# The prompt attention's side jobs laid over five tiles of the delta recursion instead of four

## What is computed

```
def dilated_attention(q, k, v, q_idx):            # mixer B, 6 heads x 64; prompt: 512 queries
    ...
        s = jnp.einsum('bqhd,bqmhd->bhqm', q, kg).astype(jnp.float32) * scale
        ...
        e = jnp.exp(s - m)
        den = jnp.sum(e, axis=-1, keepdims=True)
        outs.append(jnp.einsum('bhqm,bqmhd->bqhd', (e / den).astype(v.dtype), vg))
...
def gated_delta(q, k, v, g, beta, s0, chunk):     # mixer C, 6 heads x 64, chunks of 64 tokens
    ...
    sol = lax.linalg.triangular_solve(a_mat + jnp.eye(chunk, dtype=jnp.float32), rhs,
                                      left_side=True, lower=True, unit_diagonal=True)
    ...
    def step(s, inp):
        u_p = uu - jnp.einsum('bhcd,bhde->bhce', ww, s)
        o = jnp.einsum('bhcd,bhde->bhce', qd, s) + jnp.einsum('bhij,bhje->bhie', aa, u_p)
        s = gt[..., None, None] * s + jnp.einsum('bhcd,bhce->bhde', kd, u_p)
        return s, o
```

## Time and profile before

| | us |
|---|---|
| median of 3 runs | 1873.63 (1867.89 to 1884.23) |
| the profiled execution, its own time | 1871.8 |
| its span in the profile | 1869.9 |
| PE busy in the span | 1551.6 (83%) |
| DVE, ACT, POOL busy | 626.6, 399.7, 148.2 |

### The profile page before, as it was taken

One profiled execution on the slowest core, in us unless ns is written; L12 is line 12 of the kernel. 1 busy time (PEld: TensorE's weight loads), 2 busy tenths in 40 slices (PEclk: granted clock), 3 DMA queues, 4 the chain that ended last, 5 costly groups with the idle time before them and its releaser, 6 DMA issues. The chain is left out here.

```text
span 1869.9 us, 31394 instructions
## 1 busy us (share of the span) xinstructions
PE 1551.6 (83%) x13036; PEld 1018.1 (54%) x13036; DVE 626.6 (34%) x1625; ACT 399.7 (21%) x967; POOL 148.2 (8%) x185
## 2 busy tenths in 40 slices
PE   6999977887969798888479999788879697988882
PEld 3475666776535455444244766667765354554451
DVE  2442236665312411111234331466652133111114
ACT  3212032231511111111222210333305111111112
POOL 0000000000000022222000000000000001222210
PEclk9999888897889799999779999898969897999996
DMA  7140120002691599999701410300038825999994
GB/s 285 47 146 8 53 97 2 1 2 80 197 325 70 194 378 389 397 399 399 275 28 47 147 37 23 97 2 2 2 79 253 293 93 218 386 392 396 398 394 181
DMA packets 97261, 337.23 MB, mean 180 GB/s; under 512 B 32637, under 2 KB 44157, under 8 KB 72429
## 3 DMA queue, kind: packets, MB, share of 16 engines
q1 hardware_dynamic: 77852, 305.79, 44.8%
q0 software_dynamic: 12464, 25.92, 4.0%
q10 hardware_dynamic: 6816, 3.67, 0.7%
HBM read 313.25 MB, written 37.80 MB: 188 GB/s over the span
## 5 line engine op out<-in xcount | busy, mean ns | idle before, releaser
L1660 PE MATMUL bank<-ring,proj_raw 128*64 128x256 f32 x1536 | 202.2, 418 | 46.0 <-DMA ring<-in_w 44.4
L1401 PE MATMUL bank<-ring,hT_raw 128*128 128x384 f32 (+2 forms) x768 | 227.9, 460 | 0.0
L1401 PEld LDWEIGHTS bank<-ring,hT_raw 128*128 128x128 f32 x768 | 148.3, 194 | 77.3 <-issue 3.3
L1660 PEld LDWEIGHTS bank<-ring,proj_raw 128*64 128x64 f32 x1536 | 126.7, 145 | 106.7 <-issue 57.3
L2303 DVE TENSOR_TENSOR qkv_raw<-qkv_raw,bank 128x128 f32<-128x128 f32 x64 | 18.4, 288 | 433.1 <-ACT qkv_raw L1071 433.1
L1338 PE MATMUL bank<-hT_raw,ring 128*128 128x512 f32 x288 | 128.8, 601 | 0.0
L823 POOL DMA_INDIRECT proj_raw<-h_rows,idx x64 | 61.1, 955 | 667.1 <-DVE idx L1953 395.7
L1565 PE MATMUL bank<-ring,hT_raw 128*128 128x512 f32 x256 | 113.6, 597 | 0.0
L1117 PE MATMUL bank<-work 64*64 64x64 f32 (+1 forms) x1608 | 75.2, 261 | 37.6 <-DVE work L1805 26.2
L1117 PEld LDWEIGHTS bank<-work 64*64 64x64 f32 (+1 forms) x1608 | 68.8, 172 | 47.0 <-DVE work L1805 29.5
L1680 PE MATMUL bank<-ring,proj_raw 128*64 128x512 f32 x384 | 92.9, 604 | 1.3 <-issue 1.3
(11 more groups left out here) (323 smaller groups left out, 2162.5 us busy)
## 6 DMA issues: line engine op xcount, KB each, us to landing
ring<-in_w SPq DMA_DIRECT2D x144, 1024.0 KB, 23.0
work<-in_w SPq DMA_DIRECT2D x32, 1024.0 KB, 21.7
proj_raw<-in_w SPq DMA_DIRECT2D x16, 1024.0 KB, 29.6
ring<-in_w_in SPq DMA_DIRECT2D x10, 1536.0 KB, 16.7
ring<-in_cache_win_k SPq DMA_DIRECT2D x12, 768.0 KB, 8.7
ring<-in_cache_win_v SPq DMA_DIRECT2D x12, 768.0 KB, 11.8
ring<-in_w_out SPq DMA_DIRECT2D x4, 2048.0 KB, 22.1
proj_raw<-y_rows SPq DMA_DIRECT2D x16, 512.0 KB, 7.6
```

The costliest lines, as they stand in the source:

```text
L1401: mm = pe.matmul(bank[0:ROWS[t], 0:w.shape[2]], hT[:, k, 128 * t:128 * t + ROWS[t]], w[:, k, :], start=k == 0, stop=k == KT - 1)
L1660: mm = pe.matmul(bank[CAP * j:CAP * j + CAP, 0:256].rearrange("p (w f) -> p w f", w=2), rowsT[k % 2][:, CAP * c:CAP * c + CAP], w13[:, :, ...
```

## The change

The list of points becomes a list of pairs (tile, point): the 13 points of each of the four prompt tiles as before, then five of the sample tile (points 0, 1, 2, 3 and 10). The 33 slots are spread evenly over 57 points and not over 52. The guards that kept the side jobs out of the sample tile go, in the order of jobs and in the programs of PE, DVE and ACT.

```
--- before.py
+++ after.py
@@ -147,14 +147,14 @@
     return OUT_ORDER.index(t)
 
 
-SIDE_POINTS = tuple(range(11)) + (12, 14)
+SIDE_POINTS = [(t, n) for t in range(NP) for n in tuple(range(11)) + (12, 14)] + [(NP, n) for n in (0, 1, 2, 3, 10)]
 NSIDE = 6 + STEPS + 3
 
 
 def beside(t, point):
 
-    points = NP * len(SIDE_POINTS)
-    at = len(SIDE_POINTS) * t + SIDE_POINTS.index(point)
+    points = len(SIDE_POINTS)
+    at = SIDE_POINTS.index((t, point))
     return [n for n in range(NSIDE) if n * points // NSIDE == at]
 
 
@@ -194,20 +194,18 @@
                 v.extend(jobs[1])
         a += [("cg", t), ("D", t), ("DT", t)]
         v += [("qT", t), ("kT", t), ("bT", t)]
-        if t < NP:
-            side(0)
+        side(0)
         v += [("AA", t), ("AT0", t), ("AT1", t)]
-        if t < NP:
-            side(1)
+        side(1)
         a += [("N2", t)]
         v += [("N2T", t)]
+        side(2)
         if t < NP:
-            side(2)
             a += [("N4", t)]
             v += [("N4T", t)]
         v += [("M1", t)]
+        side(3)
         if t < NP:
-            side(3)
             a += [("N8", t)]
             v += [("M2", t)]
             side(4)
@@ -221,8 +219,8 @@
         v += [("u", t)]
         a += [("wT", t, c) for c in range(2 if t < NP else 1)]
         v += [("qdT", t)]
+        side(10)
         if t < NP:
-            side(10)
             for c in range(2):
                 v += [("wS", t, c), ("S", t, c), ("o", t, c)]
                 side(12 + 2 * c)
@@ -987,14 +985,14 @@
                     def out(label, dst, n=CW, rr=r):
                         bank = get(label)
                         act.activation(dst[0:rr, 0:n], bank[0:rr, 0:n], ACT.Copy).then_inc(s.act_drained, 1)
+                    side(t, 0)
+                    side(t, 1)
+                    out(("N2", t), N2_, CH * w)
+                    side(t, 2)
                     if t < NP:
-                        side(t, 0)
-                        side(t, 1)
-                    out(("N2", t), N2_, CH * w)
+                        out(("N4", t), N4_)
+                    side(t, 3)
                     if t < NP:
-                        side(t, 2)
-                        out(("N4", t), N4_)
-                        side(t, 3)
                         out(("N8", t), N2_)
                         side(t, 4)
                         if t:
@@ -1015,6 +1013,7 @@
                         root(o_ss)
                         act.activation(ET_[:, 0:192].rearrange("p (g n) -> p g n", g=3)[:, :, 0:NS],
                                        bank[:, 0:3 * NS].rearrange("p (g n) -> p g n", g=3), ACT.Copy).then_inc(s.act_drained, 1)
+                        side(t, 10)
 
                 act.wait_ge(s.vec_drained, V_AT[("S4", 2)] + 1)
                 for g in range(3):
@@ -1442,7 +1441,7 @@
                             pe.matmul(bank[:, 0:128 * (u + 1)], qTb[g][p0_:p0_ + 64, 128 * u:128 * u + 128],
                                       kTb[g][p0_:p0_ + 64, 0:128 * (u + 1)], start=True, stop=True).then_inc(done, 1)
                 for t in range(NT):
-                    delta_tile(pe, s, t, job, after, tr, lambda point, t=t: side(t, point) if t < NP else None)
+                    delta_tile(pe, s, t, job, after, tr, lambda point, t=t: side(t, point))
 
                 def cached(n, b):
 
@@ -2191,7 +2191,7 @@
                             dve.tensor_scalar(a_max[:, j:j + 1], a_max[:, j:j + 1], -1.0, None, ALU.mult).then_inc(s.probs_asked, 1)
                 delta_prepare(dve, s, 0, then)
                 for t in range(NT):
-                    delta_vec(dve, s, t, then, get, kept, inv_root, lambda point, t=t: side(t, point) if t < NP else None)
+                    delta_vec(dve, s, t, then, get, kept, inv_root, lambda point, t=t: side(t, point))
 
                 def own_heads(G):
```

## The result

The change makes the kernel slower: 1898.53 us (median of 4, 1896.09 to 1903.46) for 1872.42 us (median of 4), a ratio of 1.0134 with a 95% interval of 1.0100 to 1.0168. A second measurement beside the experiments gave 1.0124 (1.0090 to 1.0158). I had said 1893 us. Each ratio is to the kernel before, run beside it, and counts undisturbed executions only, which are all but three of the twelve of the kernel with 28 transposes, so it can differ a little from the ratio of the medians.

A forecast was written before the change was run, and what follows sets the result against it. It took the delta stage as bound by its chain from PE to DVE or ACT and back. Prices of 7.0 us a layer, 14 in both, plus 5 for the clock made 19 us: 1893 from the median, range 1879 to 1907.

The forecast's parts named there:

- The mechanism: Delta stage: side jobs move between free and paid places; tile 1 +2.6 us, tile 2 -0.65, tile 3 +3.9 a layer.
- The prices: Cost of a side job at each point: free at 1, 5 (tiles 1 to 3), 10; elsewhere the job less 0 to 0.7 us.
- Point 4: M2 to T: the whole job is paid, as DVE's side job stands ahead of delta_norm and waits for PE; 1.88 us.
- point 9: X to wS: the job less 0.3 us, since DVE's part stands ahead of delta_prepare; 1.4 for slot 28.
- The sample tile: Slots 31 at point 1 and 32 at point 3 cost 1.1 to 2.8 us a layer, 2.4 taken.
- the faster rival: Filled gaps keep PE at full clock in the sample tile, 10 us a layer back: 1868 us; chance 0.05.
- The clock: PE falls to half clock after long idle times: 2.5 us a layer, between -1 and 8; 5 in both.
- The rival to which I had given 0.40: The clock adds nothing, only the prices count: 1882 to 1888 us, centre 1886; chance 0.40.
- The transfers: Cache load 8 in SP's queue goes out at about 454 for 445.54, with 24 us of cover left: no cost.
- the late load: Cache load 8 comes over 24 us late, the sample attention waits and the time passes 1905 us; chance 0.01.
- made up behind: The loss is made up behind the stage, because loads of weights wait for something else: 1874 us; chance 0.05.
- The signs I had named: Tile 3 longer by 4 to 8 us, tile 2 shortest, M2 to T above 7, idle before N2 3.8, delta_norm over 1 later.

The follow-up runs named there:

- the kernel with 28 transposes: Changed kernel plus 28 identity transposes in PE's idle time at point 1 of tiles 1 and 3 and point 5 of tile 1: 1878.70 us, ratio 0.9999.
- The second trace: Trace of the changed kernel measured once more, with no edit: 1893.89 us, ratio 1.0124 to the kernel before.
- the slots at paid places: Kernel before, with the eight slots of tiles 1 to 3 each at points 2, 3, 4, 6, 7, 9, 12, 14: 1920.15 us, ratio 1.0254.
- the layout with one slot at point 5: Slots put where the chain waits anyway, with the second slot at point 5 moved away; against the kernel before: 1834.93 us, ratio 0.9818.
- two slots: Slots put where the chain waits anyway, two at once at points 1 and 5 of tiles 1 to 3; against the kernel before: 1842.64 us, ratio 0.9828.

## Why the prediction was right, point by point

**The mechanism.** Right. The kernel lost where I had said, in tiles 1 and 3, and gained in tile 2; that the sample tile or the spread as such costs is out. With the clock taken out the stages are 5.8 and 6.2 us longer than before, for the 7.0 of my sum.

**The prices.** Right within 0.8 us a tile. With the same rule (0.4 of the half time as loss) the changed kernel's tiles give bare lengths of 56.13 - 8.9 - 6.7 = 40.5 (tile 1), 47.48 - 4.65 - 2.7 = 40.1 (tile 2) and 60.54 - 8.1 - 11.6 = 40.8 (tile 3, all layer 1), the 40.4 to 40.6 of before. In layer 0 they are 39.8, 40.1 and 40.5. (The two tiles of before that the prediction leaves out, 2 and 3 of layer 0, give 40.0 and 40.4, so its agreement to 0.2 was partly luck.) Two readings are off. Point 4 costs what I said, but mostly by DVE's own work and only by a third through DVE's wait for PE. And point 9: X to wS took 1272.54 - 1265.02 = 7.52 us in tile 1 for my 5.63 + 1.4 = 7.03, so nothing of the job (1.7) is hidden there:

```profile
1265.02 0.92 PE L1116 MATMUL bank<-work 64*64 64x64 f32 x24 [0.59 <-ACT work L987]
...
1272.54 1.28 PE L1215 MATMUL bank<-state,ring 128*64 128x64 f32 x12 [3.16 <-DVE ring L1810]
```

**The sample tile.** Mis-sized: 2.4 us a layer taken, 0.3 and 2.9 measured (34.55 and 37.15 for 34.24 and 34.25), and the kernel that moves only the last two slots gained nothing and lost nothing. The second trace has the same two lengths. I had priced both slots at half clock. Where the clock stayed at half throughout (PEclk 0.50) they cost 2.9, about my upper bound of 2.8; in the other layer it came back by the end of slot 31, N2 behind it took 0.94 us for the 1.48 of before, and they cost 0.3. That is a piece of what I had given to the faster rival. The sign that I named for it, `delta_norm` begun over 1 us later, came in one layer only: counted from the tile's start 10.58 us became 10.90 in layer 0, and 10.59 became 13.51 in layer 1. So all of the longer sample tile lies ahead of `delta_norm`.

**The clock.** The term that was too small, and the step of the prediction that was furthest off. I took 2.5 us a layer. The half time of the two stages was 2 x 0.18 x 231.08 + 2 x 0.16 x 227.37 = 156 us before and 2 x 0.17 x 235.69 + 2 x 0.22 x 248.14 = 189 after; 0.4 of the difference is 13 us, with some 2 us open by PEclk's two digits, for my 5. The prices make the other 12, for my 14. So the clock was 8 us too little and the prices 2 too much. For the clock I had no better than a guess between -1 and 8 us a layer, 6.5 was measured, and that the sum still fell into the range is due to the width that I had given to this term. The rival to which I had given 0.40, that the clock adds nothing and the time is 1882 to 1888, is out, with 13 of the 25 us of the stages the clock's. Layer 0 shows no clock loss and layer 1 nearly all of it, and the other way round in the second trace, so where the clock falls stays a matter of chance. That filling a gap can take a fall away is shown; what else decides is open. One reading of mine was wrong: behind 2.53 us of idle time the clock did not come back within N2, it had never fallen. The row of that stretch has PEclk 1.00:

```profile
1333.29:1334.90 1.61, 1.61 (x48) 1.00 0.05 10
```

In layer 0 the same N2 behind the same 2.53 us took 2.47.

**The transfers.** Right. Cache load 8 went out at 456.85 (I had said 454) and at 1403.72, and the next issue at 481.79:

```profile
456.85 0.80 SPq L670 DMA_DIRECT2D hT_raw<-in_cache_win_k  x2
...
481.79 0.55 SPq L711 DMA_DIRECT2D qkv_raw<-in_w_group  x1
```

Behind the stage of layer 0 PE's waits are those of before, the longest for the values, 13.7 us after and 13.1 before (14.3 and 12.7 in layer 1):

```profile
PE bank L1508 <- DMA proj_raw<-in_cache_win_v: 13.7, 1, 13.7
```

```profile
PE bank L1509 <- DMA proj_raw<-in_cache_win_v: 13.1, 1, 13.1
```

No wait for keys appears, so the late load is out, and 25.4 us of the stages are 25.6 of the span, so nothing was made up behind them.

**The signs I had named.** Tile 3 longer by 4 to 8 us: 4.2 in layer 0, but 13.3 in layer 1, above the range, where the clock came on top. Tile 2 shorter than tiles 1 and 3: in both layers. M2 to T above 7 us in tile 3: 7.64. Idle time of 3.8 us before N2 in tiles 1 and 3: 3.79 in all four. `delta_norm` over 1 us later: in layer 1 only. The sample tile's PEclk stayed under 0.7 (0.61 and 0.50). The chances I gave to faster or made up behind found no support.

## What to carry to other kernels

When independent work is threaded through a dependent chain, an even spread is not the aim: measure for each insertion point how long the chain stands there anyway, and what the draining engine has queued behind the job, and fill the long waits first, two jobs deep where they allow it. Here the same 33 jobs cost 18 us a layer by my prices in the layout before. With the clock taken out the stages then say 24 for the change, 33 with the slots at paid places and 8 for the layout with one slot at point 5. That layout is 1.8% faster than the kernel before (0.9818, 0.9781 to 0.9855), about half of it through the places and half through the clock, which fell less often there. One more stage to put jobs in helps nothing if it moves all the others from the long waits to the short ones.

## What the runs showed of the hardware that I had not expected

- PE at full clock (PEclk 1.00 over the 28) did 16 transposes of 128 x 128 back to back in 1.97 us and 28 in 3.28, 0.12 us each, where the side jobs' groups of a few had let me expect 0.16.
- Filling PE's waits with useless work paid: 168 added transposes (28 at three places in two layers) took 15 us or more off the changed kernel's median. Of 96 small matmuls (64 x 64 by 8 columns) that began at full clock, the group still ended at half: 6.13 us, for 8.41 at half throughout.
- The same kernel spread by 36 us between executions (1862 to 1898, the one with 28 transposes), and its twelve came long and short by turns. The six longer ones (1881.82 and up) had a granted clock of 0.888 to 0.902, the six shorter ones 0.902 to 0.907. That fits the clock's falls as the source; why they alternate is open.
- Behind the same slots and the same 0.6 us of idle time N2's 48 matmuls ran at half clock in five of six tiles in one layout (2.75 to 2.83 us) and at full clock in all in another (1.61). They are the layouts with two slots and with one at point 5, which differ only in the slots of points 5, 7 and 8.
